# Latent stage: squares summed in two reduced-precision halves instead of one whole-precision product

## The chip, the cores and the metric

One NeuronCore of a Trainium2 chip runs the whole kernel. Its engines work beside each other and meet at semaphores: TensorE (PE in the profile; its weight loads are PEld), VectorE (DVE), ScalarE (ACT), GpSimd (POOL) and SyncE (SP), which here only starts transfers. The metric is the device time of one execution in microseconds.

## The reference

Two layers over a context of 256 tokens and a latent sequence of 1024: first a mixer with a short convolution and a chunked recurrent memory, then latent attention. The change touches the start of the second layer alone. There the modulated input u is projected and cut into parts, and two of the parts are normalised by their root mean square over the feature axis:

```python
def rms_norm(x, g):
    xf = x.astype(jnp.float32)
    return (xf * lax.rsqrt(jnp.mean(jnp.square(xf), axis=-1, keepdims=True) + RMS_EPS) * g).astype(x.dtype)

s_lat = split_cols(u_lat @ w_in, (384, 256, 64, 2048))   # q, kv, rope key, gate
kv = rms_norm(kv_c, kv_norm) @ w_ukv                     # context and latent tokens
q = rms_norm(q_c, q_norm) @ w_uq                         # latent tokens alone
```

## The kernel before

Activations lie transposed: features on the 128 partitions, tokens along the columns, in three chunks of tokens (`CHUNKS`: chunk 0 with 256 columns, chunks 1 and 2 with 512). So the 256 kv features are two tiles and the 384 q features three, and the mean over features needs a sum across partitions and tiles.

Precision is handled by hand. Each operand of a large product is split into a high half of the type `float32r`, a reduced-precision 32-bit type, and a low half, the rest. `mm3` (L37 to L42) makes three products: high by high, high by low, low by high. A product of plain `float32` operands is the whole-precision form.

The latent stage is laid out in the class `Latent` and in `stage_latent`. `L_WORK` is the order of TensorE's projections, each an operation (tile, chunk): (0,0) (1,0) (0,1) (1,1) (2,1) (0,2) (1,2) (2,2) (3,1) (3,2) (4,1) (4,2) (5,0) (5,1) (5,2), then the gate's tiles from (6,1) on. Tiles 0 and 1 are kv, 2 to 4 are q, 5 is the rope key. The products of one operation go into one bank out of a ring of five, and TensorE waits at `project` until the operation five places earlier has been read out of its bank.

`evacuate` lets ScalarE copy a projection from its bank into `lat_kv` or `lat_q` (L1683). ScalarE works through the operations in order too, and between them splits weights (L1664), takes the logarithm of the sums (L1887) and does the exponential and the high halves of a normalisation (`norm`, L1898 and L1902). The kv normalisation stands behind operation (3,2), ahead of the copies of (4,1) and (4,2); that of q stands behind (5,2). VectorE makes the low halves of weights (L1670) and of u (L1678), applies the normalisation (L1944, L1947), and works on the rope key and the gate tiles (L1932).

`squares` runs on GpSimd, one call for each of five groups in this order: kv chunk 0, kv chunk 1, kv chunk 2, q chunk 1, q chunk 2. It squares the first tile into an accumulator (L1721), squares each further tile into the other of two buffers (L1726) and adds it (L1728). The first group runs inside the output stage of the layer before, ahead of that stage's last two GpSimd operations (L1388, L1390) and its store (L1392); the other four follow that stage. `sq_step` counts the finished operations, and `steps_before` says how many there are ahead of a group. The squares of a later tile wait for `ss_done`, the sum of the group before, because that sum reads the buffer they write.

`sum_squares` runs on TensorE behind a fixed operation (`sum_behind`: (1,1), (0,2), (3,1), (5,1), (6,1)). It multiplies a 128 by 128 tile of ones with the accumulator (L1741), which adds up the partitions and puts the sum on each of them. `constants` fills the ones on VectorE (L1658).

Of the kernel before, what the change touches and what calls it, by code (L numbers as in the profile page):

```python
# [8 lines left out]
T = CTX + LAT  # L9
P = 128  # L10
# [15 lines left out]
F32, F32R, BF16 = mybir.dt.float32, mybir.dt.float32r, mybir.dt.bfloat16  # L26
ACT = mybir.ActivationFunctionType
ALU = mybir.AluOpType
# [3 lines left out]
def f(ap):  # L32

    return ap.bitcast(F32)
# [10 lines left out]
class Space:  # L45
# [14 lines left out]
    def sb(self, name, shape, dt=F32):  # L60
        return self.ctx.enter_context(self.nc.sbuf_tensor(f"{self.tag}_{name}", shape, dt))
# [1515 lines left out]
class Latent:  # L1577


    def __init__(self, nc, a, keep, s, at, pj, ss):  # L1580
# [4 lines left out]
        self.sums = [("kv", 0), ("kv", 1), ("kv", 2), ("q", 1), ("q", 2)]  # L1585
        self.sum_at = self.ln_at = numbered(self.sums)
        self.ss_bank = {("kv", 0): 0, ("kv", 1): 1, ("q", 1): 2, ("kv", 2): 0, ("q", 2): 1}
        self.steps_before = {("kv", 0): 0, ("kv", 1): 3, ("kv", 2): 6, ("q", 1): 9, ("q", 2): 14}
        self.sum_behind = {(1, 1): ("kv", 0), (0, 2): ("kv", 1), (3, 1): ("kv", 2), (5, 1): ("q", 1), (6, 1): ("q", 2)}
        self.group_end = {"kv": (1, 2), "q": (4, 2)}  # L1590
        self.last_of = {t: max(self.done_at[op] for op in L_WORK if op[0] == t) for t in range(len(L_TILES))}
# [2 lines left out]
        def sb(name, shape, where, dt=F32):  # L1594
            return over(nc, f"l_{name}", shape, dt, where)

        self.u_hi, self.u_lo, self.u_raw = {}, {}, {}
        for j, k in self.pieces:
            hi, lo = at[f"u{j}"][2 * k:2 * k + 2]
# [7 lines left out]
        x = at["lat"]  # L1607
# [1 line left out]
        x += 8 * T + 4096  # L1609
        self.rms_q, self.rms_kv, self.kr = sb("rms_q", [P, LAT], x), sb("rms_kv", [P, T], x + 4 * LAT), sb("kr", [DR, T], x + 4 * LAT + 4 * T)  # L1610
        self.lat_q = sb("lat_q", [P, 3, LAT], x + 4 * LAT + 8 * T)
        self.ones = sb("ones", [P, P], at["ones"])
        x = at["lq"]
        keep["lq"] = sb("lq_hi", [P, 3, LAT], x, F32R), sb("lq_lo", [P, 3, LAT], x + 12 * LAT, F32R)
        x = at["lkv"]
# [4 lines left out]
        x = kv_lo + 8 * T + 8 * LAT + 512  # L1620
# [34 lines left out]
        sp.dma_start(self.u_raw[(j, k)][:, :], self.u_src[k][:, self.span(j)]).then_inc(self.u_in[(j % 2, k)], 16)  # L1655

    def constants(self, dve):
        self.nc.vector.memset(self.ones[:, :], 1.0).then_inc(self.set_ok, 1)  # L1658
        self.nc.vector.memset(self.eps[:, :], RMS_EPS).then_inc(self.set_ok, 1)

    def w_high(self, act, t):
# [48 lines left out]
    def squares(self, pool, group):  # L1710

        g, (kind, j) = self.sum_at[group] - 1, group
        n, tiles, step = CHUNKS[j][1], range(2) if kind == "kv" else range(2, 5), self.steps_before[group]
        acc, part = self.sq[g % 2][:, 0:n], self.sq[1 - g % 2][:, 0:n]
        for x, t in enumerate(tiles):
            lat = self.lat_of((t, j))
            pool.wait_ge(self.free_a, self.a_free[(t, j)])
            if step:
                pool.wait_ge(self.sq_step, step)
            if x == 0:  # L1720
                pool.tensor_tensor(acc, lat, lat, ALU.mult).then_inc(self.sq_step, 1)  # L1721
                step += 1
                continue
            if x == 1 and g:
                pool.wait_ge(self.ss_done, g)
            pool.tensor_tensor(part, lat, lat, ALU.mult).then_inc(self.sq_step, 1)  # L1726
            pool.wait_ge(self.sq_step, step + 1)
            pool.tensor_tensor(acc, acc, part, ALU.add).then_inc(self.sq_step, 1)  # L1728
            step += 2

    def sum_squares(self, pe, group):
        g, (kind, j) = self.sum_at[group], group
        n = CHUNKS[j][1]
        if g == 1:
            pe.wait_ge(self.set_ok, 2)
        pe.wait_ge(self.sq_step, self.steps_before[group] + (3 if kind == "kv" else 5))
        if group == ("kv", 2):
            pe.wait_ge(self.ln_ok, self.ln_at[("kv", 0)])
        if group == ("q", 2):
            pe.wait_ge(self.ln_ok, self.ln_at[("kv", 1)])  # L1740
        self.nc.tensor.matmul(self.ss[self.ss_bank[group]][:, 0:n], self.ones[:, :], self.sq[(g - 1) % 2][:, 0:n], start=True,  # L1741
                              stop=True).then_inc(self.ss_done, 1)


class HeadWeights:
# [784 lines left out]
def over(nc, name, shape, dt, offset):  # L2530

    return nc.alloc_sbuf_tensor_at(name, shape, dt, offset=offset)
# [20 lines left out]
def layout(inputs):  # L2553

    arrays = {n: np.ascontiguousarray(x) for n, x in inputs.items() if n not in ("x", "ctx", "ev_conv_w")}
    arrays["conv_t"] = np.ascontiguousarray(np.asarray(inputs["ev_conv_w"])[0].T)
    arrays["h0"] = np.concatenate([np.asarray(inputs["ctx"])[0], np.asarray(inputs["x"])[0]])
    for n in ("od_q_norm", "od_kv_norm"):
        arrays[n] = np.ascontiguousarray(arrays[n].reshape(-1, P).T)
    arrays["mod_b_col"] = np.ascontiguousarray(np.asarray(inputs["mod_b"])[:, 0:2 * D].reshape(2, 2 * KD, P).transpose(2, 0, 1))  # L2560
    arrays["ln_col"] = np.stack([np.asarray(inputs[n])[0].reshape(KD, P).T for n in ("ln_g", "ln_b")], axis=1)
    arrays.update(constants())
    return arrays
# [55 lines left out]
```

## Time and profile before

| | |
|---|---|
| median of 3 runs | 2867.58 us (2866.63 to 2867.74) |
| profiled execution | 2864.85 us, of which span 2863.1 us |
| TensorE busy | 2829.3 us (99%), mean granted clock 0.998 |
| TensorE weight loads | 2430.1 us (85%) |
| VectorE, ScalarE | 1543.3 us (54%), 1185.2 us (41%) |
| GpSimd | 285.7 us (10%) |

Times on the timeline are microseconds from the first instruction. The latent stage's projections start in the output stage of the first layer, near 1478 us. A group of instructions is written as line, engine, operation, output<-inputs with the program's names; `l_sq` are the buffers of the squares, `l_ones` the ones. The names e_pj, e_x, e_y, e_z and e_e are the banks that the projections and sums are written to. What stands in brackets behind a row is how long the engine had been idle before it, and what ended that. TensorE's records overlap: the ends of matmuls are modelled, and the distance from one start to the next is what one costs.

### The profile page before, as it was taken

What the parts mean: (1) busy time and instruction counts of PE and PEld (TensorE: products, weight loads), DVE (VectorE), ACT (ScalarE), POOL (GpSimd) and SP (SyncE); (2) the same over time, 40 slices, a digit from 0 to 9 for tenths busy, and PEclk for the clock granted to TensorE, in tenths of its full rate; (3) what the DMA queues carried; (4) which work ended last, traced back from release to release, by engine and by line L of the source; (5) the groups of instructions that cost most, each with busy time, mean ns of one, the idle gap of its engine ahead of it and who ended that gap; (6) DMA issues with size and microseconds to landing.
All of it is one profiled execution on the core that took longest, in us unless ns stands there. A gap on an engine that the chain in (4) does not pass through costs nothing. (4 is left out here: it accounts for less than half of the span.)

```text
span 2863.1 us, 38077 instructions
## 1 busy us (share of the span) xinstructions
PE 2829.3 (99%) x15377; PEld 2430.1 (85%) x15377; DVE 1543.3 (54%) x2793; ACT 1185.2 (41%) x1979; POOL 285.7 (10%) x298
## 2 busy tenths in 40 slices
PE   7999999999999999999999999999999999999998
PEld 5888888888888888888887888888888888888886
DVE  6646554555366536654353325666666666666544
ACT  6323322332233223342243315666666666666500
POOL 5100000000000000001232001202202022020000
PEclk9999999999999999999999999999999999999999
DMA  7311130113111311163361320010000100002332
GB/s 211 100 34 47 47 122 26 53 49 114 32 47 47 116 39 48 45 217 103 111 196 51 126 81 34 27 35 23 28 26 27 38 20 32 26 24 103 126 102 75
DMA packets 221504, 200.76 MB, mean 70 GB/s; under 512 B 12085, under 2 KB 193221, under 8 KB 221330
## 3 DMA queue, kind: packets, MB, share of 16 engines
q1 hardware_dynamic: 208578, 184.91, 20.9%
q0 software_dynamic: 2352, 8.17, 0.8%
q10 hardware_dynamic: 10400, 5.24, 0.6%
q8 instruction: 123, 2.02, 0.3%
q14 instruction: 51, 0.42, 0.0%
HBM read 157.34 MB, written 40.95 MB: 69 GB/s over the span
## 5 line engine op out<-in xcount | busy, mean ns | idle before, releaser
L40 PE MATMUL e_pj<-e_u_hi,e_w_hi 128*128 128x512 f32 (+1 forms) x864 | 307.9, 356 | 1.0 <-PEq L58 1.0
L40 PE MATMUL e_pj<-e_u_hi,v_w_hi 128*128 128x512 f32 (+1 forms) x864 | 307.7, 356 | 0.2 <-DVE v_kk_lo L882 0.2
L41 PE MATMUL e_pj<-e_u_lo,e_w_hi 128*128 128x512 f32 (+1 forms) x864 | 306.0, 354 | 0.0
L41 PE MATMUL e_pj<-e_u_lo,v_w_hi 128*128 128x512 f32 (+1 forms) x864 | 306.0, 354 | 0.0
L42 PE MATMUL e_pj<-e_u_hi,v_w_lo 128*128 128x512 f32 (+1 forms) x864 | 305.8, 354 | 0.0
L42 PE MATMUL e_pj<-e_u_hi,e_w_lo 128*128 128x512 f32 (+1 forms) x864 | 305.7, 354 | 0.0
L2241 ACT CAST t_pt_hi<-t_ring 128x512 fp32r<-128x512 f32 (+1 forms) x384 | 181.4, 519 | 232.3 <-PE t_ring L2447 232.3
L2330 DVE TENSOR_TENSOR t_pt_lo<-t_ring,t_pt_hi 128x512 fp32r<-128x512 f32 (+1 forms) x384 | 216.0, 597 | 52.6 <-ACT t_pt_hi L2241 50.9
L2257 ACT ACTIVATE t_prob<-t_scores,t_bias 128x1280 f32<-128x1280 f32 x128 | 170.6, 1333 | 87.7 <-DVE t_bias L2351 87.5
L42 PEld LDWEIGHTS e_pj<-e_u_hi,v_w_lo 128*128 128x128 f32 x864 | 163.2, 189 | 23.2
L42 PEld LDWEIGHTS e_pj<-e_u_hi,e_w_lo 128*128 128x128 f32 x864 | 163.1, 189 | 23.1
L40 PEld LDWEIGHTS e_pj<-e_u_hi,v_w_hi 128*128 128x128 f32 x864 | 163.3, 189 | 22.4 <-issue 0.9
L40 PEld LDWEIGHTS e_pj<-e_u_hi,e_w_hi 128*128 128x128 f32 x864 | 163.2, 189 | 22.1 <-issue 1.2
L41 PEld LDWEIGHTS e_pj<-e_u_lo,v_w_hi 128*128 128x128 f32 x864 | 163.4, 189 | 20.7
L41 PEld LDWEIGHTS e_pj<-e_u_lo,e_w_hi 128*128 128x128 f32 x864 | 163.2, 189 | 20.4
L2262 ACT ACTIVATE t_prob<-t_prob,t_rec 128x1280 f32<-128x1280 f32 x128 | 177.0, 1382 | 7.4 <-DVE t_rec L2355 7.4
L2447 PEld LDWEIGHTS t_ring<-k_ident,t_prob 128*128 128x128 f32 x1280 | 147.2, 140 | 16.7
L2447 PE MATMUL t_ring<-k_ident,t_prob 128*128 128x128 f32 x1280 | 160.3, 272 | 0.0
L656 POOL TENSOR_TENSOR v_wgt<-v_wgt,v_mask 128x128 f32<-128x128 f32 x80 | 41.3, 519 | 1039.2 <-DMA v_wgt<-r_rows 1039.0
L40 PE MATMUL t_scores<-t_kn_hi,t_qn_hi 128*128 128x256 f32 x381 | 140.3, 368 | 2.0 <-ACT t_prob L2257 2.0
L41 PE MATMUL t_scores<-t_kn_lo,t_qn_hi 128*128 128x256 f32 x381 | 135.6, 356 | 0.0
L2500 PE MATMUL t_scores<-l_kr_lo,t_qs 128*128 128x256 f32 x381 | 135.6, 356 | 0.0
(500 smaller groups left out, 6700.2 us busy)
## 6 DMA issues: line engine op xcount, KB each, us to landing
e_w_raw<-in_ev_w_in SPq DMA_DIRECT2D x72, 512.0 KB, 4.7
v_mw<-in_mod_w SPq DMA_DIRECT2D x32, 512.0 KB, 3.7
l_w_raw<-in_od_w_in SPq DMA_DIRECT2D x21, 512.0 KB, 3.9
o_m_raw<-mixT SPq DMA_DIRECT2D x20, 512.0 KB, 5.4
o_w_raw<-in_ev_w_out SPq DMA_DIRECT2D x16, 512.0 KB, 8.8
zgT<-l_lat_q SPq DMA_DIRECT2D x16, 512.0 KB, 3.8
t_zg<-zgT SPq DMA_DIRECT2D x32, 256.0 KB, 2.8
ogT<-t_zg SPq DMA_DIRECT2D x32, 256.0 KB, 2.0
```

Source lines behind the costliest of these rows:

```text
L40: nc.tensor.matmul(out, whi, xhi, start=first, stop=False)
L41: nc.tensor.matmul(out, whi, xlo, start=False, stop=False)
L42: return nc.tensor.matmul(out, wlo, xhi, start=False, stop=last)
L656: pool.tensor_tensor(wgt[d][x][:, :], wgt[d][x][:, :], mask[:, d, :], ALU.add).then_inc(masked, 1)
L2241: nc.scalar.copy(dst, src).then_inc(ring_hi, 1)
L2257: nc.scalar.activation(prob[x][:, :], S[:, 0:T], ACT.Exp, bias=bias[x][:, :], accum_out=total[x][:, :]).then_inc(exp_ok, 1)
L2262: nc.scalar.mul(prob[x][:, :], prob[x][:, :], rec[x][:, :]).then_inc(prob_ok, 1)
L2330: nc.vector.tensor_tensor(dst, src, hi, ALU.subtract).then_inc(ring_free, frees(op))
L2447: last = nc.tensor.transpose(ps[:, c * P:(c + 1) * P], prob[t % 2][:, (c0 + c) * P:(c0 + c + 1) * P], ident[:, :])
L2500: last = nc.tensor.matmul(out, qs[b][:, tok], kr2[1][:, k0:k0 + n], start=False, stop=True)
```

## The change

GpSimd gets two more operations at the end of each group. The first multiplies the accumulator by the first column of the ones, repeated, and writes the product as `float32r`: the high half. The second subtracts that from the accumulator: the low half. The halves go into the same bytes as the two square buffers (`sq_r` has the addresses of `sq`): the high half over the partial squares, the low half over the accumulator. So the first square of a group now waits for `ss_done`, where before the second one did. The ones become `float32r`, and TensorE makes two products of that type, high then low, into one bank, in place of one product of whole precision. The step numbers are adapted: 5 in place of 3 for a kv group, 7 in place of 5 for a q group.

```diff
--- before.py
+++ after.py
@@ -1585,7 +1585,7 @@
         self.sums = [("kv", 0), ("kv", 1), ("kv", 2), ("q", 1), ("q", 2)]
         self.sum_at = self.ln_at = numbered(self.sums)
         self.ss_bank = {("kv", 0): 0, ("kv", 1): 1, ("q", 1): 2, ("kv", 2): 0, ("q", 2): 1}
-        self.steps_before = {("kv", 0): 0, ("kv", 1): 3, ("kv", 2): 6, ("q", 1): 9, ("q", 2): 14}
+        self.steps_before = {("kv", 0): 0, ("kv", 1): 5, ("kv", 2): 10, ("q", 1): 15, ("q", 2): 22}
         self.sum_behind = {(1, 1): ("kv", 0), (0, 2): ("kv", 1), (3, 1): ("kv", 2), (5, 1): ("q", 1), (6, 1): ("q", 2)}
         self.group_end = {"kv": (1, 2), "q": (4, 2)}
         self.last_of = {t: max(self.done_at[op] for op in L_WORK if op[0] == t) for t in range(len(L_TILES))}
@@ -1609,7 +1609,8 @@
         x += 8 * T + 4096
         self.rms_q, self.rms_kv, self.kr = sb("rms_q", [P, LAT], x), sb("rms_kv", [P, T], x + 4 * LAT), sb("kr", [DR, T], x + 4 * LAT + 4 * T)
         self.lat_q = sb("lat_q", [P, 3, LAT], x + 4 * LAT + 8 * T)
-        self.ones = sb("ones", [P, P], at["ones"])
+        self.sq_r = [sb(f"sq_r{i}", [P, 512], at["lat"] + 8 * T + 2048 * i, F32R) for i in range(2)]
+        self.ones = sb("ones", [P, P], at["ones"], F32R)
         x = at["lq"]
         keep["lq"] = sb("lq_hi", [P, 3, LAT], x, F32R), sb("lq_lo", [P, 3, LAT], x + 12 * LAT, F32R)
         x = at["lkv"]
@@ -1655,7 +1656,7 @@
         sp.dma_start(self.u_raw[(j, k)][:, :], self.u_src[k][:, self.span(j)]).then_inc(self.u_in[(j % 2, k)], 16)
 
     def constants(self, dve):
-        self.nc.vector.memset(self.ones[:, :], 1.0).then_inc(self.set_ok, 1)
+        self.nc.vector.memset(f(self.ones[:, :]), 1.0).then_inc(self.set_ok, 1)
         self.nc.vector.memset(self.eps[:, :], RMS_EPS).then_inc(self.set_ok, 1)
 
     def w_high(self, act, t):
@@ -1718,28 +1719,36 @@
             if step:
                 pool.wait_ge(self.sq_step, step)
             if x == 0:
+                if g:
+                    pool.wait_ge(self.ss_done, g)
                 pool.tensor_tensor(acc, lat, lat, ALU.mult).then_inc(self.sq_step, 1)
                 step += 1
                 continue
-            if x == 1 and g:
-                pool.wait_ge(self.ss_done, g)
             pool.tensor_tensor(part, lat, lat, ALU.mult).then_inc(self.sq_step, 1)
             pool.wait_ge(self.sq_step, step + 1)
             pool.tensor_tensor(acc, acc, part, ALU.add).then_inc(self.sq_step, 1)
             step += 2
+        hi, lo = self.sq_r[1 - g % 2][:, 0:n], self.sq_r[g % 2][:, 0:n]
+        pool.wait_ge(self.sq_step, step)
+        if g == 0:
+            pool.wait_ge(self.set_ok, 1)
+        pool.tensor_tensor(hi, acc, f(self.ones[:, 0:1]).broadcast_to([P, n]), ALU.mult).then_inc(self.sq_step, 1)
+        pool.wait_ge(self.sq_step, step + 1)
+        pool.tensor_tensor(lo, acc, f(hi), ALU.subtract).then_inc(self.sq_step, 1)
 
     def sum_squares(self, pe, group):
         g, (kind, j) = self.sum_at[group], group
         n = CHUNKS[j][1]
         if g == 1:
             pe.wait_ge(self.set_ok, 2)
-        pe.wait_ge(self.sq_step, self.steps_before[group] + (3 if kind == "kv" else 5))
+        pe.wait_ge(self.sq_step, self.steps_before[group] + (5 if kind == "kv" else 7))
         if group == ("kv", 2):
             pe.wait_ge(self.ln_ok, self.ln_at[("kv", 0)])
         if group == ("q", 2):
             pe.wait_ge(self.ln_ok, self.ln_at[("kv", 1)])
-        self.nc.tensor.matmul(self.ss[self.ss_bank[group]][:, 0:n], self.ones[:, :], self.sq[(g - 1) % 2][:, 0:n], start=True,
-                              stop=True).then_inc(self.ss_done, 1)
+        out, lo, hi = self.ss[self.ss_bank[group]][:, 0:n], self.sq_r[(g - 1) % 2][:, 0:n], self.sq_r[g % 2][:, 0:n]
+        self.nc.tensor.matmul(out, self.ones[:, :], hi, start=True, stop=False)
+        self.nc.tensor.matmul(out, self.ones[:, :], lo, start=False, stop=True).then_inc(self.ss_done, 1)
 
 
 class HeadWeights:
```

## Rows read from the trace of the kernel before

**Rows 1.** The page: busy us, share of the span, instructions of each engine

```profile
PE 2829.3 (99%) x15377; PEld 2430.1 (85%) x15377; DVE 1543.3 (54%) x2793; ACT 1185.2 (41%) x1979; POOL 285.7 (10%) x298
```

**Rows 2.** Waits from 1480 to 1600 us: engine line, waited for, total, times, longest

```profile
PEld e_e L1741 <- POOL l_sq L1728: 0.4, 1, 0.4
```

**Rows 3.** Timeline around the second sum: start us, us, engine, line, operation

```profile
1506.83 0.39 PE L42 MATMUL e_y<-l_u_hi,l_w_lo 128*128 128x512 f32 x1
...
1507.06 1.02 PE L1741 MATMUL e_x<-l_sq,l_ones 128*128 128x512 f32 x2
...
1508.15 0.40 PE L41 MATMUL e_pj<-l_u_lo,l_w_hi 128*128 128x512 f32 x1
```

**Rows 4.** TensorE's timeline at the first sum, then at the third

```profile
1495.70 0.59 PE L1741 MATMUL e_pj<-l_sq,l_ones 128*128 128x256 f32 x2
...
1496.37 0.40 PE L41 MATMUL e_pj<-l_u_lo,l_w_hi 128*128 128x512 f32 x1
...
1524.29 1.02 PE L1741 MATMUL e_pj<-l_sq,l_ones 128*128 128x512 f32 x2
```

**Rows 5.** GpSimd's timeline: squares and additions

```profile
1486.28 2.85 POOL L1388 TENSOR_TENSOR o_h_out<-o_y,o_ln_g 128x1024 f32<-128x1024 f32 x1
...
1497.89 1.03 POOL L1721 TENSOR_TENSOR l_sq<-l_lat_kv 128x512 f32<-128x512 f32 x1 [4.41 <-DMA h<-o_h_out]
1500.05 1.53 POOL L1726 TENSOR_TENSOR l_sq<-l_lat_kv 128x512 f32<-128x512 f32 x1 [1.13 <-ACT l_lat_kv L1683]
1501.65 1.63 POOL L1728 TENSOR_TENSOR l_sq<-l_sq,l_sq 128x512 f32<-128x512 f32 x1
...
1515.39 1.29 POOL L1728 TENSOR_TENSOR l_sq<-l_sq,l_sq 128x512 f32<-128x512 f32 x1
...
1525.48 1.04 POOL L1726 TENSOR_TENSOR l_sq<-l_lat_q 128x512 f32<-128x512 f32 x1 [7.62 <-PE e_pj L1741]
...
1543.90 1.87 POOL L1726 TENSOR_TENSOR l_sq<-l_lat_q 128x512 f32<-128x512 f32 x1 [16.02 <-ACT l_lat_q L1683]
1545.85 1.29 POOL L1728 TENSOR_TENSOR l_sq<-l_sq,l_sq 128x512 f32<-128x512 f32 x1
1547.29 1.84 POOL L1721 TENSOR_TENSOR l_sq<-l_lat_q 128x512 f32<-128x512 f32 x1
```

**Rows 6.** GpSimd by line and form, 57.2 to 65.1 us: busy us, mean ns

```profile
L194 POOL TENSOR_TENSOR e_u_lo<-m_u_raw,e_u_hi 128x512 fp32r<-128x512 f32 x2 | 2.5, 1271 | 4.3 <-DVE m_u_raw L280 4.3
```

**Rows 7.** GpSimd by line and form: the whole trace

```profile
L194 POOL TENSOR_TENSOR e_u_lo<-m_u_raw,e_u_hi 128x512 fp32r<-128x512 f32 x8 | 22.1, 2761 | 31.2 <-DVE m_u_raw L280 31.2
```

**Rows 8.** VectorE's timeline beside them

```profile
1498.38 6.66 DVE L1678 TENSOR_TENSOR l_u_lo<-l_u_raw,l_u_hi 128x512 fp32r<-128x512 f32 x7 [1.37 <-ACT l_u_hi L1674]
...
1546.78 1.45 DVE L1670 TENSOR_TENSOR l_w_lo<-l_w_raw,l_w_hi 128x1024 fp32r<-128x1024 f32 x1 [1.91 <-ACT l_w_hi L1664]
```

**Rows 9.** ScalarE's timeline ahead of the fourth sum

```profile
1534.70 1.05 ACT L1664 CAST l_w_hi<-l_w_raw 128x1024 fp32r<-128x1024 f32 x1 [3.29 <-DMA l_w_raw<-in_od_w_in]
...
1543.24 0.58 ACT L1683 COPY l_lat_q<-e_y 128x512 f32<-128x512 f32 x1
```

**Rows 10.** TensorE's timeline at the fourth sum and at the fifth

```profile
1546.83 0.39 PE L1705 MATMUL e_z<-l_u_hi,l_w_hi 128*128 128x512 f32 x1
...
1547.20 1.13 PE L1741 MATMUL e_e<-l_sq,l_ones 128*128 128x512 f32 x2
...
1557.30 1.02 PE L1741 MATMUL e_x<-l_sq,l_ones 128*128 128x512 f32 x2
```

**Rows 11.** TensorE's timeline at the first gated tile's bank

```profile
1580.31 0.47 PE L40 MATMUL e_y<-l_u_hi,l_w_hi 128*128 128x512 f32 x1 [0.19 <-DVE l_lat_q L1932]
```

**Rows 12.** TensorE early: an idle stretch; then windows: length, busy, granted clock, DMA

```profile
20.65 0.37 PE L328 MATMUL e_z<-m_w_hi,m_cs 128*4 128x256 f32 x1 [4.25 <-DVE m_w_lo L265]
...
19.40:19.80 0.40, 0.00 (x0) 0.50 1.13 353
...
25.50:26.00 0.50, 0.50 (x4) 0.50 1.11 350
```

## The prediction

> **What bounds the kernel now.** I read the page's busy shares first: TensorE is busy for 2829.3 of 2863.1 us [rows 1]. A change anywhere else counts only if it makes TensorE wait, and every product that TensorE is spared counts at its pitch. Then the waits of the stretch 1480 to 1600 us, in which all five sums of squares lie. TensorE waits for the chain of squares once, 0.4 us on its weight loads, at the fourth sum [rows 2]. Then the timelines around the sums. After a projection product of 512 columns the next instruction starts 0.23 us later (0.2275 over many), although the record says 0.39, because the records overlap [rows 3]. So I cost TensorE's work from start to start, not by duration.
>
> **What a sum costs TensorE now.** A whole-precision product shows as two records. At the second sum the last product before it starts at 1506.83, the sum at 1507.06, and the second projection product after it at 1508.15 [rows 3]. Taking one pitch (0.23) off, the first projection product takes its place at 1507.92, so the sum holds TensorE for 1507.92 - 1507.06 = 0.86 us. At the first sum, of 256 columns, the same reading gives 1496.37 - 0.23 - 1495.70 = 0.44 us [rows 4].
>
> **What the new sum costs.** Two products of the reduced-precision type at the projection pitch: 2 x 0.2275 = 0.455 us for 512 columns; half of that, 0.23 us, is my estimate for 256. The saving is 0.405 us at each of four sums and 0.21 at the first: 1.83 us in all, every bit of it on the path as long as no wait takes it back. The type conversion of the ones costs nothing: the same memset, 36 us before its first use. Bounds: products of this type with weights that need their own load already run at this pitch in the rows, so I see no reason for a cost above 0.86 (no saving) or below 0.455.
>
> **What GpSimd gets.** Two operations more per sum. No row of before shows a multiply by a repeated column. Nearest rows: a square, which reads one tile twice, takes 1.04 us when it is alone, at 1525.48 [rows 5]; the addition of two tiles takes 1.29 [rows 5]; and a subtraction that writes the reduced-precision type takes 1.27 [rows 6]. I take 1.29 for each, with 0.08 to 0.12 us between dependent ones, so about 2.7 us per sum of 512 columns. Bounds alone: 1.04 and 2.76 us, that same line's mean over the whole trace, where most of its operations lie beside long ones of VectorE [rows 7]. GpSimd and VectorE hold each other up: the square at 1547.29 took 1.84 us while a VectorE subtraction of two tiles ran from 1546.78 [rows 5, 8], 0.8 us longer than alone. The Trainium skill, "SBUF — State Buffer", section "SBUF: two separate sides", says that the pair of ports shared by the two is an exclusive lock held for a whole instruction; by that rule a new operation placed there pays up to the rest of one VectorE operation (here those 0.8 us) and not a slowdown in proportion. By a proportional slowdown (1.84/1.04) the fourth sum would be later by 0.2 us and nothing else would change.
>
> Sum by sum:
> - First (256 columns): two operations of about 0.65 to 1.06 us are put ahead of the layer's last output rows on GpSimd. Its end at 1486.3 [rows 5] moves to about 1488.1, nine microseconds ahead of TensorE's use at 1495.70. What is queued behind it is the multiply at 1486.28, its addition, and the store. The next square waited for that store and started at 1497.89 [rows 5]; it moves to about 1499.7. SyncE's rope load waits for the same store, and its next weight load is not due before 1507. No cost here.
> - Second: squares, addition and split now run one behind the other from 1499.7, beside VectorE's seven subtractions that last until 1505.0 [rows 8]. With 1.03, 1.53, 1.63 as in the rows, then 1.63 and 1.29 and gaps, the low half is there at about 1507.2. TensorE asks at 1506.85 (0.21 earlier than now). I take 0.3 us of waiting; bounds 0 and 1.2.
> - Third: the addition ends at 1516.7 and the split at 1519.4. TensorE asks at 1523.9 [rows 4]. Hidden, with 4.5 us of cover. The first square of the fourth group now has to stand behind the third sum, since its buffer is the one TensorE reads; it goes from 1516.8 to 1524.5. The next square waited until 1525.48 anyway, and the group's last tile arrives at 1543.8. Hidden.
> - Fourth, **the one that decides**. The last tile of the group is copied by ScalarE from 1543.24, at the end of a chain that starts when TensorE finishes a projection and a weight load lands, 1534.70 [rows 9]. GpSimd squares it from 1543.90, and adds from 1545.85 to 1547.14 [rows 5]. TensorE arrives at 1546.83 + 0.23 = 1547.06 and starts at 1547.20 [rows 10]. So the cover is already used up. Now comes: gap 0.12, 0.8 behind VectorE's subtraction, 1.29, gap 0.08, 1.29, that is 3.5 us: 1550.65. Both sides of this race start from TensorE's own progress, so earlier savings move both. The wait is 1550.65 - 1547.06 = 3.6 us where it was 0.14: +3.45. Bounds: +1.9 (1.04 for the multiply and no blocking) and +5.0 (both at 1.87, the longest square of these rows [rows 5], and both blocked).
> - Fifth: counted from R, the point at which TensorE goes on after the fourth sum (now 1547.20 + 0.86 = 1548.06), TensorE asks at R + 9.24 [rows 10]. GpSimd can start only when the fourth sum is done, about R + 0.5 (today 1.2 us after a sum's start [rows 4, 5]), and has 3 squares, 2 additions and 2 split operations: 3.1 + 2.6 + 2.6 + 0.5 of gaps = 8.8, ready at R + 9.35. A wait of 0.1 us, at most 1.3. But this one is given back: at 1580.31, 32.25 us after R, TensorE waits 0.2 us for VectorE's first gated tile [rows 11], which hangs on the normalisation of q and so on R. The fifth saving (0.4) only makes that wait 0.6 us, and a wait at the fifth sum of up to 0.6 us is taken out of it again.
>
> **The sum**, in the profiled execution's own terms (span 2863.1, run 2864.85; the runs' median, 2867.58, is 2.7 above it, and I add the difference to that median):
> savings ahead of R: -0.21 - 3 x 0.405 = -1.43; waits: +0.3 + 3.45 = +3.75; fifth saving and fifth wait: 0 at the ring wait. Net **+2.3 us**, 2867.6 + 2.3 = **2869.9**. Later stages stay as they are: they hang on TensorE's progress, and no wait of theirs that I found is on a clock of its own. The bounds together give +0.4 to +5.5 without any change of TensorE's clock.
>
> **Rivals.**
> 1. The clock falls in the new gap. Early in the kernel TensorE stood idle for 4.25 us from 16.4, had its clock at 0.50 (1.2 GHz) by 19.4, and kept it for about five microseconds of the work that began at 20.65 [rows 12]. The new gap is about 3.4 us long, a little more than that 3 us. Price: between half of 3.4 us of work and half of 5.3 us, +1.7 to +2.7, total +4.0 to +5.0: 2871.6 to 2872.6. Against it: the work before the gap is dense here, and it was sparse there. The Trainium skill, "TensorE: Matmul & The Clock Gate", section "What's actually happening", says that idleness sends the clock to half and sustained work brings it back, which is what those rows show. Chance 0.17.
> 2. The gap does not appear, because the chain ahead of it turns out shorter or TensorE arrives later: then only the savings are left, -1.8 at best and -1.4 if the fifth is lost at the ring wait: 2865.8 to 2866.2. The profile speaks against it: the 0.4 us of waiting for GpSimd is there today. Chance 0.09.
> 3. **Slower** beyond what can be told apart: the repeated-column multiply or the reduced-precision writes are slow on GpSimd. At 2.76 us each, the mean of the early 512-column operations [rows 7], the fourth wait grows by 3 us, the second by 3, and the fifth, beyond its 0.6 of cover, by about 2: +2.3 + 8 = +10, 2878. It decides from about 1.9 us per new operation: each extra 0.1 us costs about 0.6 in all, so the net reaches 5.7 us. Against it are the 1.27 us rows of the same output type. Chance 0.08, some of it from a fallen clock on top.
> 4. The change does not make the sums cheaper (two reduced-precision products hold TensorE as long as the two records do now): -1.43 goes, net +3.7, 2871.3. Against it: the pitch of every projection product. Chance 0.03.
>
> **How the numbers follow.** The forecast has 0.60 with its own span 2868.0 to 2872. Of this kernel a measurement tells about 0.2% from no change, 5.7 us. Forecast, rivals 1, 2 and 4 lie inside that: 0.89, less 0.01 for the overlap with the upper bounds: same 0.88. Slower 0.09: rival 3 and the corner of slow operations with a fallen clock. Faster 0.03: only what I overlooked. The range for 8 in 10 takes in the forecast, most of rival 1 and the upper part of rival 2: 2866.2 to 2873.6.
>
> **What would show it.** In the profile after: sums of two products 0.23 us apart; TensorE waiting for the split's subtraction before the fourth sum, about 3.5 us, and at most about a microsecond before the second and the fifth; none before the first and third; the new operations at 1.3 us alone and about 2.1 where VectorE runs; granted clock 1.00 between 1545 and 1560 (0.50 there is rival 1). The prediction is wrong if the fourth wait is below 2 or above 5 us, or if a wait appears outside 1495 to 1585 us.

## The result and the profile after

Eleven runs of each kernel: the changed one 2872.54 us (2871.27 to 2874.73), the one before 2866.97 us (2864.93 to 2868.25). The ratio is 1.0021 with a 95% interval of 1.0013 to 1.0029: slower by 5.6 us, clear of the interval, and just at the 0.2% that I called the limit. The profiled execution has a span of 2872.9 us. That is 9.8 above the span before; 2.4 of these lie ahead of the first sum and 1.4 behind the wait at the first gated tile, and both turn up in traces of other kernels of this study, whose medians don't follow them. So everything below is read from distances between marks of one trace.

The page, span and first line, to be read against [rows 1]:

```profile
span 2872.9 us, 38088 instructions
...
PE 2833.4 (99%) x15377; PEld 2433.0 (85%) x15377; DVE 1547.4 (54%) x2793; ACT 1184.9 (41%) x1979; POOL 296.9 (10%) x308
```

GpSimd has 11 us more work and TensorE 4 us more busy time, though its products got cheaper: a first hint at a slower clock. TensorE's waits between 1490 and 1570 us (engine, line, waited for, total, times, longest), where before there was only [rows 2]:

```profile
PEld e_e L1750 <- POOL l_sq_r L1737: 3.8, 1, 3.8
PE e_e L1750 <- POOL l_sq_r L1737: 3.4, 1, 3.4
...
PE e_y L40 <- DVE l_u_lo L1679: 1.2, 2, 0.7
...
PE e_x L1750 <- POOL l_sq_r L1737: 0.2, 1, 0.2
```

The wait for the fourth sum's split is there, 3.4 us on TensorE's own row. One is new that I did not forecast: that for the low halves of u. The one at the second sum, 0.2 us, is small only because TensorE comes late. TensorE's timeline at the sums, and at the first gated tile; the answers to [rows 3, 4, 10, 11]:

```profile
1498.10 0.28 PE L1750 MATMUL e_pj<-l_sq_r,l_ones 128*128 128x256 f32 x1
...
1509.11 0.50 PE L40 MATMUL e_y<-l_u_hi,l_w_hi 128*128 128x512 f32 x1 [0.72 <-DVE l_u_lo L1679]
...
1511.70 0.50 PE L1750 MATMUL e_x<-l_sq_r,l_ones 128*128 128x512 f32 x1 [0.18 <-POOL l_sq_r L1737]
1512.04 0.40 PE L1751 MATMUL e_x<-l_sq_r,l_ones 128*128 128x512 f32 x1
...
1528.61 0.39 PE L1750 MATMUL e_pj<-l_sq_r,l_ones 128*128 128x512 f32 x1
1528.83 0.39 PE L1751 MATMUL e_pj<-l_sq_r,l_ones 128*128 128x512 f32 x1
...
1554.45 0.79 PE L1750 MATMUL e_e<-l_sq_r,l_ones 128*128 128x512 f32 x1 [3.37 <-POOL l_sq_r L1737]
1555.04 0.63 PE L1751 MATMUL e_e<-l_sq_r,l_ones 128*128 128x512 f32 x1
...
1565.47 0.39 PE L1750 MATMUL e_x<-l_sq_r,l_ones 128*128 128x512 f32 x1
1565.69 0.39 PE L1751 MATMUL e_x<-l_sq_r,l_ones 128*128 128x512 f32 x1
...
1588.66 0.47 PE L40 MATMUL e_y<-l_u_hi,l_w_hi 128*128 128x512 f32 x1 [0.82 <-DVE l_lat_q L1941]
```

The two products of a sum of 512 columns start 0.22 to 0.23 us apart at the third and the fifth (1528.61, 1528.83), 0.34 at the second, which starts out of a wait, and 0.59 at the fourth, out of a wait and at the lower clock. GpSimd's timeline, the answer to [rows 5]:

```profile
1497.26 0.62 POOL L1392 DMA_DIRECT2D h<-o_h_out  x1 [0.30 <-POOL o_h_out L1390]
1504.13 1.24 POOL L1724 TENSOR_TENSOR l_sq<-l_lat_kv 128x512 f32<-128x512 f32 x1 [6.25 <-DMA h<-o_h_out]
...
1508.59 1.37 POOL L1735 TENSOR_TENSOR l_sq_r<-l_sq,l_ones 128x512 fp32r<-128x512 f32 x1
1510.04 1.61 POOL L1737 TENSOR_TENSOR l_sq_r<-l_sq,l_sq_r 128x512 fp32r<-128x512 f32 x1
...
1521.08 1.04 POOL L1735 TENSOR_TENSOR l_sq_r<-l_sq,l_ones 128x512 fp32r<-128x512 f32 x1
1522.19 1.29 POOL L1737 TENSOR_TENSOR l_sq_r<-l_sq,l_sq_r 128x512 fp32r<-128x512 f32 x1
...
1549.78 1.30 POOL L1729 TENSOR_TENSOR l_sq<-l_sq,l_sq 128x512 f32<-128x512 f32 x1
1551.16 1.90 POOL L1735 TENSOR_TENSOR l_sq_r<-l_sq,l_ones 128x512 fp32r<-128x512 f32 x1
1553.14 1.26 POOL L1737 TENSOR_TENSOR l_sq_r<-l_sq,l_sq_r 128x512 fp32r<-128x512 f32 x1
```

Alone, the multiply by the repeated column takes 1.04 us and the subtraction 1.29 (at 1521.08 and 1522.19); at the fourth sum the multiply takes 1.90 beside VectorE. GpSimd waits 6.25 us for the store to land, where it was 4.41. And TensorE's granted clock around the fourth sum (stretch, length, busy, clock, DMA share, GB/s):

```profile
1553.60:1554.00 0.40, 0.00 (x0) 0.86 0.00 0
1554.00:1555.00 1.00, 0.55 (x1) 0.50 0.00 0
...
1557.40:1558.00 0.60, 0.60 (x4) 1.00 0.00 0
```

The mean of 0.86 over 1553.60 to 1554.00 puts the fall to 0.50 (1.2 GHz) at about 1553.9, 2.8 us after TensorE's last product had ended. It was at 1.00 (2.4 GHz) again at 1557.3, 2.8 us after work had begun.

**The distances** that the rest rests on, in us between the first products of the sums, and from the fifth sum to the wait at the first gated tile. Each number is the difference of two starts in TensorE's timeline of one trace.

| kernel | 1st to 2nd | 2nd to 3rd | 3rd to 4th | 4th to 5th | 5th to gated tile | sum | median us |
|---|---|---|---|---|---|---|---|
| before | 11.36 | 17.23 | 22.91 | 10.10 | 23.01 | 84.6 | 2866.97 |
| before_again | 11.39 | 17.22 | 22.93 | 10.11 | 23.29 | 84.9 | 2867.16 |
| changed | 13.60 | 16.91 | 25.84 | 11.02 | 23.19 | 90.6 | 2872.54 |
| after_again | 12.90 | 16.91 | 25.73 | 11.26 | 23.17 | 90.0 | 2873.19 |
| split_alone | 13.89 | 17.31 | 26.29 | 12.87 | 23.20 | 93.6 | 2875.28 |
| products_alone | 11.14 | 16.78 | 22.41 | 9.71 | 23.19 | 83.2 | 2866.13 |
| fill_gap | 12.68 | 16.91 | 26.00 | 9.71 | 23.17 | 88.5 | 2871.78 |
| first_whole | 13.17 | 16.78 | 25.88 | 12.48 | 23.29 | 91.6 | 2873.13 |
| second_whole | 12.18 | 17.23 | 25.72 | 11.30 | 23.18 | 89.6 | 2872.57 |
| fourth_whole | 13.76 | 16.91 | 22.47 | 10.10 | 23.07 | 86.3 | 2869.66 |
| third_only | 11.36 | 17.22 | 22.55 | 10.11 | 23.18 | 84.4 | 2866.55 |
| store_first | 11.14 | 16.78 | 25.76 | 9.70 | 23.16 | 86.5 | 2871.49 |
| wait_moved | 13.86 | 16.79 | 25.89 | 9.72 | 23.20 | 89.5 | 2873.02 |
| one_product | 11.02 | 16.55 | 22.25 | 9.47 | 23.21 | 82.5 | 2865.39 |

The changed kernel is 5.4 to 6.0 us longer over these marks in its two traces, which is the 5.6 us of the medians. The loss lies in three places: first to second sum (+1.5 to +2.2), third to fourth (+2.8 to +2.9), fourth to fifth (+0.9 to +1.2).

### The profile page after: what moved, and what is told of

Read it like the earlier page. It is cut to its first block and busy times, and to the rows that moved or that the text cites. A ratio compares the mean times of both kernels' runs of the same rounds, so it can differ in the third digit from the quotient of the medians.

```text
span 2872.9 us, 38088 instructions
## 1 busy us (share of the span) xinstructions
PE 2833.4 (99%) x15377; PEld 2433.0 (85%) x15377; DVE 1547.4 (54%) x2793; ACT 1184.9 (41%) x1979; POOL 296.9 (10%) x308
## 5 line engine op out<-in xcount | busy, mean ns | idle before, releaser
L2266 ACT ACTIVATE t_prob<-t_scores,t_bias 128x1280 f32<-128x1280 f32 x128 | 170.5, 1332 | 89.6 <-DVE t_bias L2360 89.4
```

Source lines behind the costliest of these rows:

```text
L2266: nc.scalar.activation(prob[x][:, :], S[:, 0:T], ACT.Exp, bias=bias[x][:, :], accum_out=total[x][:, :]).then_inc(exp_ok, 1)
```

## The experiments

**Theory** after the first trace: the wait for the fourth split costs what was forecast; the clock, fallen in that wait, costs some 1.5 us more; and the second sum is late, for a cause to be found. **Rivals**: the reduced-precision products cost more than they seem to; the first trace was an odd one; the fallen clock is hidden behind the gated tile.

### after_again: the changed kernel once more

> The changed kernel once more, as the yardstick of this group and for a second trace. Theory (the new wait ahead of the fourth sum, then the clock at half, then a late second sum): TensorE idle 3.4 to 3.8 us ahead of the fourth sum; granted clock 0.50 for some 3 us around it in this profile too; median +4.5 to +7 us against the kernel before. Rival (the first trace was an odd one, the change is worth the forecast +2.3): clock at 1.00 around the fourth sum and median +1.5 to +3.5.

2873.19 us, ratio 1.0027 (1.0016 to 1.0039) to the kernel before. Idle ahead of the fourth sum 3.25 us on TensorE's row, a little under the 3.4 to 3.8 expected, the clock at 0.50 around it, first to second sum 12.90. The first trace was not an odd one.

### before_again: the kernel before once more

> The kernel before once more, for a second trace: first to second sum 11.2 to 11.6 us, fourth sum to fifth 10.1, from the first sum to the wait at the first gated tile 84.6 within 0.5. If these vary by a microsecond by themselves, the distances can't carry the readings made of them.

11.39, 17.22, 22.93, 10.11 us: the four distances between sums repeat within 0.03 us. The last one varies by 0.3 (the wait at the gated tile was 0.47 us long here, 0.19 in the first trace). Distances can carry tenths, where a ratio of ten runs has an interval of two to three microseconds either way.

### split_alone: GpSimd's part without the cheaper products

```diff
-        self.nc.tensor.matmul(out, self.ones[:, :], hi, start=True, stop=False)
-        self.nc.tensor.matmul(out, self.ones[:, :], lo, start=False, stop=True).then_inc(self.ss_done, 1)
+        self.nc.tensor.matmul(out, f(self.ones[:, :]), f(hi), start=True, stop=True).then_inc(self.ss_done, 1)
```

> GpSimd's two new operations and all waits as in the change, but TensorE makes one whole-precision product of the high half in place of two reduced-precision ones (the low half is left out of the sum). It prices the GpSimd part by itself. Theory: all the loss lies here, so +1.2 to +1.8 us on top of the changed kernel, minus the fifth sum's 0.4 that the ring wait takes anyway: +6 to +8 against the kernel before. Rival (the reduced-precision products, with their own weight loads, are what costs): equal to the kernel before or within 1.5 us of it.

2875.28 us, ratio 1.0033 (1.0021 to 1.0046), +8.4 in the median and +8.9 over the marks. All the loss comes with the split, and the rival that put it on the products has fallen. The median is a little above my 6 to 8, because the clock cost more here: fourth to fifth sum 12.87 us, 2.8 more than before, and it was back at 1.00 only 5.8 us after work began.

### products_alone: the cheaper products without the split

```diff
-            pool.tensor_tensor(acc, acc, part, ALU.add).then_inc(self.sq_step, 1)
+            out = self.sq_r[g % 2][:, 0:n] if x == len(tiles) - 1 else acc
+            pool.tensor_tensor(out, acc, part, ALU.add).then_inc(self.sq_step, 1)
...
-        self.nc.tensor.matmul(self.ss[self.ss_bank[group]][:, 0:n], self.ones[:, :], self.sq[(g - 1) % 2][:, 0:n], start=True,
-                              stop=True).then_inc(self.ss_done, 1)
+        out, hi = self.ss[self.ss_bank[group]][:, 0:n], self.sq_r[(g - 1) % 2][:, 0:n]
+        self.nc.tensor.matmul(out, self.ones[:, :], hi, start=True, stop=False)
+        self.nc.tensor.matmul(out, self.ones[:, :], hi, start=False, stop=True).then_inc(self.ss_done, 1)
```

> The kernel before with two reduced-precision products per sum and no split: the last addition writes the reduced-precision type and both products read it (the low half is left out, the high half is counted twice). Theory: the products are the gain, 0.405 us at four sums and 0.21 at the first, of which the fourth waits for GpSimd as before and the fifth ends in the ring wait: -1.0 to -1.6 us against the kernel before, which a total may not show; in the trace, from the first sum's start to the first gated tile's wait the distance shrinks by 1.0 to 1.6 us. Rival: the products cost as much as one whole-precision product, distance unchanged.

TensorE's timeline at the third sum, the gated tile's wait behind it:

```profile
1525.06 0.39 PE L1744 MATMUL e_pj<-l_sq_r,l_ones 128*128 128x512 f32 x1
1525.28 0.39 PE L1745 MATMUL e_pj<-l_sq_r,l_ones 128*128 128x512 f32 x1
...
1580.37 0.47 PE L40 MATMUL e_y<-l_u_hi,l_w_hi 128*128 128x512 f32 x1 [0.81 <-DVE l_lat_q L1935]
```

1.4 us less over the marks (83.2 against 84.6), 2866.13 us, ratio 0.9998 (0.9989 to 1.0007). The products are worth what the pitch said, 0.4 us at a sum of 512 columns. The last distance, 23.19, holds the cheaper fifth sum and is still no shorter than before (23.01 and 23.29): the wait at the gated tile is 0.81 us where it was 0.19 and 0.47. The fifth saving is not to be had. The sums of this kernel are not those of the reference, since it takes the high half twice and leaves the low half out; it is there for the time alone.

### fill_gap: work in the idle stretch

```diff
+        if group == ("q", 1):
+            for i in range(14):
+                self.nc.tensor.matmul(self.ss[2][:, 0:512], self.w_hi[5 % L_SLOTS][:, i % KD, :], self.u_hi[(1, i % KD)][:, :], start=True, stop=True)
         pe.wait_ge(self.sq_step, self.steps_before[group] + (5 if kind == "kv" else 7))
```

> The changed kernel with 14 projection products of 512 columns put on TensorE ahead of its wait for the fourth sum; they write the bank that the sum then overwrites. They take 3.2 us at full clock, less than the idle stretch of 3.6 us, so they delay nothing by themselves. Theory (the clock falls in the gap and costs about 1.7 us): granted clock 1.00 from 1545 to 1565, median 1.2 to 2.2 us below the changed kernel. Rival (the fallen clock is hidden by the wait at the first gated tile): median equal to the changed kernel within 0.5 us, and that wait longer by as much as was gained.

The sum's row with its rest of waiting, and the clock:

```profile
1553.78 0.50 PE L1753 MATMUL e_e<-l_sq_r,l_ones 128*128 128x512 f32 x1 [0.32 <-POOL l_sq_r L1737]
...
1552.00:1554.00 2.00, 1.68 (x8) 1.00 0.00 0
1554.00:1556.00 2.00, 2.00 (x10) 1.00 0.00 0
```

The clock stays at 1.00. Third to fourth sum is 26.00, 0.2 to 0.3 more than in the changed kernel, so the filling delays little, and fourth to fifth is 9.71 where the changed kernel had 11.02 and 11.26. The wait at the gated tile is not longer (0.76 against 0.82 and 0.79), so the rival falls: the clock's 1.3 to 1.6 us are not hidden, and from the third sum to the fifth the filled kernel is 1.2 and 1.3 us shorter. The median, 2871.78 (ratio 1.002, 1.0011 to 1.0029), is 0.8 and 1.4 below the two of the changed kernel, where 1.2 to 2.2 was expected; that alone would prove little.

### fourth_whole: the fourth sum as before

Its group is not split, and one whole-precision product sums it; steps and waits follow.

```diff
+        self.split = [("kv", 0), ("kv", 1), ("kv", 2), ("q", 2)]
...
+            if g and x == (0 if self.sums[g - 1] in self.split else 1):
+                pool.wait_ge(self.ss_done, g)
...
+        if group not in self.split:
+            return
         hi, lo = self.sq_r[1 - g % 2][:, 0:n], self.sq_r[g % 2][:, 0:n]
```

> The changed kernel, but the fourth group alone is neither split nor multiplied in halves. Theory: TensorE's idle stretch ahead of the fourth sum is back to 0.1 to 0.4 us, third to fourth sum 22.4 to 22.6 us (25.8 in the changed kernel, 22.9 before), fourth to fifth 10.1, clock at 1.00 all through; median 3.5 to 5 us below the changed kernel's, that is +0.5 to +2 against the kernel before. Rival (TensorE would be held up there in another way, by ScalarE's copy or the fifth group's squares): third to fourth or fourth to fifth longer than in the kernel before.

The gap is gone: third to fourth sum 22.47 us, fourth to fifth 10.10, clock at 1.00. Over the marks 86.3, 3.7 to 4.3 less than the changed kernel; the median 2869.66 (ratio 1.0008, 0.9999 to 1.0017) is 2.9 less, under the 3.5 that I expected at least. The fourth split with the clock is the larger part of the loss.

### What makes the second sum late: store_first, wait_moved, first_whole, second_whole

The split of the first group puts the last store of the output stage back behind two more GpSimd operations, and it now goes out in the middle of the loads of u for the last chunk. Three suspects: the store and the loads slow each other; GpSimd's second group starts late, since it waits for the store; GpSimd's two more operations of the second group stand in the way of VectorE's low halves of u.

**store_first** puts the whole first group behind the issue of the store:

```diff
-                    if n == count - 1:
-                        latent.squares(pool, ("kv", 0))
                     pool.tensor_tensor(h_out[b][:, :], y[b][:, :], ln_g[:, :], ALU.mult).then_inc(gain_ok, 1)
...
                     pool.dma_start(result[m], h_out[b][:, :]).then_inc(y_out[b], 16)
+                    if n == count - 1:
+                        latent.squares(pool, ("kv", 0))
```

> The changed kernel with the whole first group, squares and split, behind the issue of the last store instead of ahead of its operations. Both theories of the second sum's delay expect it gone if the store's time is the cause: store issued about 2.6 us earlier than in the kernel before relative to the first projections, first to second sum 11.1 to 11.6 with its own small saving; a wait before the first sum of at most 1 us is possible, as the group ends just ahead of it. If the second sum is still over 12.3 after the first, the store is not the cause.

First to second sum 11.14 us, the same as with the products alone: the delay is gone with all splits in place. The store went out 3.1 us before the first of those loads (in the kernel before 0.2 after it, in the changed one 1.8 after). It landed in 3.8 us by the view of transfers, and the loads in 4.4. That view in the kernel before, the changed one and store_first (1490 to 1512 us; size, then median from issue to landing):

```profile
l_u_raw<-u1T SPq DMA_DIRECT2D x8, 256.0 KB, 4.8
...
l_u_raw<-u1T SPq DMA_DIRECT2D x8, 256.0 KB, 6.3
...
l_u_raw<-u1T SPq DMA_DIRECT2D x8, 256.0 KB, 4.4
h<-o_h_out POOLq DMA_DIRECT2D x1, 512.0 KB, 3.8
```

The first sum started 37.5 us after the ones were set, 36.8 in the kernel before. The group's own lateness is not the cause of these 0.8 us: its low half was ready at 1499.01 and the sum started at 1500.96. TensorE's weight loads waited 1.0 us for the low halves of u for chunk 1, because VectorE's four subtractions took 7.31 us beside GpSimd's output rows (3.88 in the kernel before):

```profile
PEld e_z L40 <- DVE l_u_lo L1679: 1.0, 2, 0.5
...
1487.35 7.31 DVE L1679 TENSOR_TENSOR l_u_lo<-l_u_raw,l_u_hi 128x512 fp32r<-128x512 f32 x4
```

Counted from the ones, the second sum comes at 48.7 us, against 48.2 and 48.3 in the kernel before and 50.9 and 49.7 in the changed one, so most of the delay is gone by this reading too. The median is 2871.49, ratio 1.0016 (1.0007 to 1.0026), 4.5 above the kernel before, 4.9 above the runs of that kernel beside it. The marks and the late first sum explain 2.7 of that; no trace shows where the rest lies.

**wait_moved** lets GpSimd's wait for its last stores stand behind the squares:

```diff
-            if layer == 0:
-                for b in range(2):
-                    pool.wait_ge(y_out[b], 16 * (LAT // P // 2))
...
             for group in SUMS[1:]:
                 latent.squares(pool, group)
+            for stored in tail["stored"]:
+                pool.wait_ge(*stored)
```

> The changed kernel with GpSimd's wait for its last stores put behind the squares, so the second group no longer stands behind the store; the store and the loads of u still meet. Theory (what is late at the second sum is mainly the transfers that slow each other): TensorE still waits for low halves of u, first to second sum 12.3 or more. Rival (only GpSimd's wait for the store is late): first to second sum back to 11.0 to 11.5.

GpSimd's second group in it, and ScalarE beside it:

```profile
1497.42 1.03 POOL L1721 TENSOR_TENSOR l_sq<-l_lat_kv 128x512 f32<-128x512 f32 x1 [0.98 <-PE e_pj L1748]
1503.40 1.06 POOL L1724 TENSOR_TENSOR l_sq<-l_lat_kv 128x512 f32<-128x512 f32 x1 [4.95 <-ACT l_lat_kv L1681]
...
1501.48 1.35 ACT L1672 CAST l_u_hi<-l_u_raw 128x512 fp32r<-128x512 f32 x2 [2.96 <-DMA l_u_raw<-u1T]
1502.74 0.58 ACT L1681 COPY l_lat_kv<-e_z 128x512 f32<-128x512 f32 x1
1503.21 2.24 ACT L1672 CAST l_u_hi<-l_u_raw 128x512 fp32r<-128x512 f32 x4
```

The first square now starts at 1497.42, but the second waits 4.95 us for a tile that ScalarE copies at 1502.74, behind high halves of u for whose load it had waited 2.96 us (1501.48). First to second sum 13.86: no gain. The loads took 6.3 us here too, 6.0 to 6.7 in all kernels in which the store was issued 1.0 to 1.8 us after the first of them, and 4.8 to 5.2 where it was issued within 0.4 us of it. So in this trace the second sum is late without GpSimd's wait for the store: the loads are late, and with them the low halves of u, for which TensorE waited three times, 1.8 us in all. In fill_gap it was GpSimd's wait: the loads took 5.1 us there and TensorE waited for no low half of u, but the store took 6.8, GpSimd's second group began at 1504.17, and TensorE stood idle for its split:

```profile
1510.87 0.50 PE L1753 MATMUL e_x<-l_sq_r,l_ones 128*128 128x512 f32 x1 [1.38 <-POOL l_sq_r L1737]
```

That the store and the loads slow each other is read from these times; no run moves the loads alone.

**first_whole** leaves the first group unsplit and whole (the other four as changed):

```diff
+        if g == 0:
+            return
         hi, lo = self.sq_r[1 - g % 2][:, 0:n], self.sq_r[g % 2][:, 0:n]
...
+        if g == 1:
+            self.nc.tensor.matmul(self.ss[self.ss_bank[group]][:, 0:n], f(self.ones[:, :]), self.sq[0][:, 0:n], start=True, stop=True).then_inc(self.ss_done, 1)
+            return
```

> The changed kernel, but the first group is neither split nor multiplied in halves, so GpSimd's output rows and their store go out when they did before. Theory (the store that moved back by two operations runs into the loads of u and takes 6 to 7 us in place of 4.4, which delays the squares and the low halves of u): store to landing back to about 4.4 us, first to second sum 11.2 to 11.6 us (11.36 in the kernel before, 12.7 to 13.6 in the changed one), no wait for low halves of u; the rest as in the changed kernel; median 1 to 2 us below the changed one. Rival (the second group's own two operations are too long for the stretch): first to second sum stays above 12.5.

```profile
PE e_y L40 <- DVE l_u_lo L1679: 1.2, 2, 0.7
...
1494.24 0.61 POOL L1392 DMA_DIRECT2D h<-o_h_out  x1 [0.30 <-POOL o_h_out L1390]
1500.86 1.03 POOL L1724 TENSOR_TENSOR l_sq<-l_lat_kv 128x512 f32<-128x512 f32 x1 [6.00 <-DMA h<-o_h_out]
...
1554.00:1556.00 2.00, 2.00 (x6) 0.50 0.03 8
1556.00:1558.00 2.00, 2.00 (x6) 0.50 0.00 0
1558.00:1560.00 2.00, 2.00 (x8) 0.77 0.00 0
```

This missed: 13.17 us, and the store took 6.00 us though nothing was put ahead of it. In this trace SyncE started the loads of u 1.0 us before the store was issued, and no run shows why; in the two traces of the kernel before the store and the first load were issued within 0.2 us of each other, and the store landed in 4.4 and 4.3. So the split of the first group is not needed for a slow store. The clock stayed low for about 6 us of work here, till nearly 1559, and fourth to fifth sum took 12.48 us.

**second_whole** leaves the second group unsplit and whole, with the same edit as fourth_whole:

```diff
+        self.split = [("kv", 0), ("kv", 2), ("q", 1), ("q", 2)]
```

> The changed kernel, but the second group alone is neither split nor multiplied in halves. Theory (GpSimd's two extra operations in the stretch where VectorE makes the low halves of u hold those up, and come late themselves): first to second sum 11.3 to 11.6 us, no or nearly no wait for low halves of u, though the last store lands as late as in the changed kernel; the low-half subtractions end by 10.4 us after the first sum. Rival (the loads of u are late by themselves once the store has moved): first to second sum 12.5 or more.

```profile
1507.16 0.50 PE L40 MATMUL e_y<-l_u_hi,l_w_hi 128*128 128x512 f32 x1 [0.72 <-DVE l_u_lo L1680]
...
1509.35 1.02 PE L1753 MATMUL e_x<-l_sq,l_ones 128*128 128x512 f32 x2
...
1501.67 6.64 DVE L1680 TENSOR_TENSOR l_u_lo<-l_u_raw,l_u_hi 128x512 fp32r<-128x512 f32 x6 [2.97 <-ACT l_u_hi L1676]
```

12.18 us, between what the two theories expected. The store landed after 6.14 us, the low halves of u were done at 1508.3, 11.1 us after the first sum, and TensorE waited 0.7 us for them. In third_only, with the second group whole too, the store took 5.72 us, the low halves were done 9.8 us after the first sum, and nothing was lost (11.36). In the changed kernel they were done 12.4 us after it:

```profile
1504.79 5.72 DVE L1679 TENSOR_TENSOR l_u_lo<-l_u_raw,l_u_hi 128x512 fp32r<-128x512 f32 x4 [0.31 <-ACT l_u_hi L1675]
...
1550.62 1.53 DVE L1671 TENSOR_TENSOR l_w_lo<-l_w_raw,l_w_hi 128x1024 fp32r<-128x1024 f32 x1 [1.82 <-ACT l_w_hi L1665]
```

Four subtractions in 5.72 us: 1.43 each, where seven took 0.95 each before [rows 8] and six 1.11 each in second_whole, whose loads were as late but whose second group has no split. Both causes matter, then, and together they cost more than each alone: late loads with the second group whole cost 0.8 us, an undisturbed store with the second group split costs next to nothing (store_first), and the two together 1.3 to 2.5 (fill_gap, 12.68, to split_alone, 13.89).

### third_only: the one split that is free

```diff
+        self.split = [("kv", 2)]
```

> Only the third group is split and multiplied in halves, the one whose split is hidden for 4 us; the other four sums are as in the kernel before. Theory: second to third sum 17.2 as before, third to fourth 0.4 us shorter (22.5), all others as before; median 0.4 us below the kernel before, which the total can't tell from no change. Rival: the split costs something there too, first to last distance not below the kernel before.

Second to third 17.22, third to fourth 22.55 (22.91 and 22.93 before): the saving of 0.4 us is there and nothing else has moved. The low half is ready 5.1 us ahead of the sum. The median, 2866.55 (ratio 1.0001, 0.9992 to 1.001), can't show the saving.

### one_product: no low half at all

Against products_alone:

```diff
-        self.nc.tensor.matmul(out, self.ones[:, :], hi, start=True, stop=False)
-        self.nc.tensor.matmul(out, self.ones[:, :], hi, start=False, stop=True).then_inc(self.ss_done, 1)
+        self.nc.tensor.matmul(out, self.ones[:, :], hi, start=True, stop=True).then_inc(self.ss_done, 1)
```

> The kernel before with the last addition writing the reduced-precision type and a single product of it per sum: no split, and the low half is left out of the sum. Theory: each sum of 512 columns costs 0.23 us in place of 0.86; four of five savings count (the fifth ends in the wait at the first gated tile): -0.3 -3 x 0.63 = -2.2 us from the first sum to that wait, and about -2 in the median, 0.9993 of the kernel before. Rival: a sum's place in the order costs a fixed time whatever its type, distance within 1.5 us of the kernel before.

82.5 us over the marks, 2.1 to 2.4 less than the kernel before, and a median of 2865.39, 1.8 below its runs; the ratio, 0.9994 (0.9985 to 1.0003), leaves no change possible. It is the fastest of all, and its sum is of lower precision. None of the versions that keep both halves is shown to beat the kernel before.

## Why the prediction was right or wrong

The range (2866.2 to 2873.6) holds the 2872.54 us, but not for the forecast's reasons alone: of +5.6 us the forecast had +2.3, its own span ended at 2872, and rival 1 with +4.0 to +5.0 was nearer. That the time lies inside rival 1's 2871.6 to 2872.6 is partly luck: 1.5 to 2.2 us of it come from the second sum, which rival 1 did not have. Point by point:

- **What a sum costs, before and after**: right. 0.405 us of saving per sum of 512 columns; products_alone and third_only show 0.36 to 0.5.
- **The new operations**: right within 0.25 us. The multiply alone takes 1.04 us, not 1.29, like a square; the subtraction 1.29. At the fourth sum 1.90 and 1.26, forecast 2.09 (1.29 and 0.8 of being held up; measured 1.04 and 0.86) and 1.29, and the longer one was held up by a VectorE operation that ran from 1550.62, as said. Rival 3 (2.76 us each) did not come.
- **The fourth sum**: right. Third to fourth sum was to grow by 3.45 - 0.4 = 3.05 us; it grew by 2.9 and 2.8. The bounds given for this wait do not follow from their own terms, which make about +2.4 and +5.4 and not +1.9 and +5.0; the measured growth lies inside either pair.
- **The fifth sum**: right. No wait, and its saving ends at the gated tile, where the wait is 0.8 us now. In fill_gap, where the clock doesn't disturb the reading, 32.3 us pass from R to the gated tile, as before.
- **The first and third**: right, no wait.
- **The second sum: the step that failed.** I moved the squares by the two added operations (about 1.8 us) and took the store's 4.4 us and VectorE's end at 1505.0 as fixed. The store took 6.0 to 7.1 us in the kernels that split the first group and keep the order, the loads of u that ScalarE and VectorE wait for came late, and GpSimd's longer group stretched VectorE's subtractions. Term forecast: 0.3 - 0.2 = +0.1 us between first and second sum. Measured: +2.2, +1.5, and +1.3 to +2.5 over all kernels that split both groups and keep the order. I had asked when GpSimd would be ready for TensorE, and which transfers wait for the store. I had not asked which run beside it, or what GpSimd's longer group does to the low halves of u that TensorE needs.
- **The clock: a chance that was too low.** 0.17 for a gap of 3.4 us. Seven traces have an idle gap of 3.2 to 3.4 us there. In five of them the clock fell to 0.50 (the changed kernel twice, split_alone, first_whole, second_whole). It did not fall in store_first and wait_moved, with gaps of the same length, and there fourth to fifth sum is 9.70 and 9.72. The price was 1.3 to 1.6 us in three traces (11.02, 11.26 and 11.30 against 9.71), and 2.8 in two (12.48 against 9.71, 12.87 against 10.10); forecast 1.7 to 2.7. As the forecast had it, the price is about half of the work done at the lower clock: 2.8, 3.4 and 3.3 us of it in the first three, 6.0 and 5.8 in the other two. The Trainium skill, "TensorE: Matmul & The Clock Gate", section "What's actually happening", says that idleness sends the clock to half and that work brings it back; these traces agree, and they show that an idle stretch of 3.2 to 3.4 us was enough in five traces of seven.

The sum with what was measured: -0.3 (third), 2.2 or 1.5 (second), 2.9 or 2.8 (fourth), 0.9 or 1.2 (fifth with clock), 0 to 0.2: 5.4 to 6.0 us. The chance of 0.88 for "within 0.2%" was too high: the time came out at the edge.

**Open**: how the 1.3 to 2.5 us at the second sum divide between late transfers and longer subtractions, since both change from trace to trace with the moment at which SyncE starts its loads; where some 2 us of store_first's median lie; and why the clock falls in some executions and not in others.

## What to carry to other kernels

On an engine that is 99% busy, half a microsecond saved at a product is worth less than one elementwise operation more in the chain that feeds it: look for the sum whose input is ready last, and change only those whose input has been waiting (here the third, 5 us ahead). When operations are added to an engine, follow everything that is queued behind them: a store that goes out two operations later can meet the loads of the next stage. An idle stretch of some 3.4 us in TensorE's work has to be priced with a fallen clock, 1.3 to 2.8 us on top here, and filling it with products that nobody needs took back 1.2 to 1.3 us of it.

## What the runs showed of the hardware that was not expected

- A multiply by one column repeated over 512 columns costs GpSimd 1.04 us, as much as squaring one tile, where an addition or subtraction of two tiles costs 1.29.
- A store of 512 KB from GpSimd's queue landed 4.3 to 4.6 us after its issue when it went out within 0.4 us of the first of SyncE's eight loads of u, in four traces; issued 0.8 us after that one it took 5.7 in one trace, and issued 1.0 to 2.4 us after it 6.0 to 7.1, in seven traces.
- VectorE's four subtractions that make low halves of u (512 columns) took 3.3 to 3.9 us in the output stage in three traces, and 7.31 us in store_first, where GpSimd's two 1024-column operations began 0.2 us behind them.
- With gaps of 3.2 to 3.4 us on TensorE's row, the granted clock fell in five of seven traces; it fell 2.4 to 3.2 us after the last product had ended in four, and 4.4 us after it, when work had already begun again, in second_whole. It was back 2.8, 3.4, 4.4, 5.8 and 6.0 us after work began.
